# q's sums of squares taken by ones-column products on TensorE in place of transposes, in a gated delta rule layer

## What is computed

```python
qkv = jax.nn.silu(causal_depthwise_conv(qkv, w_conv_qkv[i]))      # 4 taps
q, k, v = jnp.split(qkv, 3, axis=-1)
q, k, v = l2norm(heads(q)), l2norm(heads(k)), heads(v)
o_a = gated_delta_chunked(q, k, v, g_log, beta)

def l2norm(x):
    return x * lax.rsqrt(jnp.sum(x * x, axis=-1, keepdims=True) + EPS)
```

## Time and profile before

| | |
|---|---|
| median of 3 runs | 2480.13 us (2479.77 to 2482.06) |
| the profiled execution | 2482.13 us, its span 2480.6 us |
| busy in the span: PE, PEld | 2424.2 us (98%), 1992.7 us (80%) |
| DVE, ACT, POOL | 1605.1 us (65%), 1152.9 us (46%), 142.3 us (6%) |
| instructions | 34230 |
| phase QKVZ | from about 481 to 984 us of the span |

### The profile page before, as it was taken

One profiled execution on the slowest core, in us unless ns is written; L12 is line 12 of the kernel. 1 busy time (PEld: TensorE's weight loads), 2 busy tenths in 40 slices (PEclk: granted clock), 3 DMA queues, 4 the chain that ended last, 5 costly groups with the idle time before them and its releaser, 6 DMA issues.

```text
span 2480.6 us, 34230 instructions
## 1 busy us (share of the span) xinstructions
PE 2424.2 (98%) x13427; PEld 1992.7 (80%) x13427; DVE 1605.1 (65%) x2181; ACT 1152.9 (46%) x1497; POOL 142.3 (6%) x259
## 2 busy tenths in 40 slices
PE   7999999999999999999999999999999999999998
PEld 6878878787778777778888788888888888888886
DVE  5799999777676766655656655655555544555554
ACT  5444444474353535343455564545444444443443
POOL 3000000011010102010000000000000000000000
PEclk9999999999999999999999999999999999999999
DMA  7566666556343435557655565656565656685563
GB/s 238 182 215 199 203 198 217 165 192 196 120 162 120 161 120 179 196 192 279 209 185 200 165 201 177 204 171 211 170 212 170 228 187 197 195 283 189 187 221 118
DMA packets 227756, 472.22 MB, mean 190 GB/s; under 512 B 12537, under 2 KB 13410, under 8 KB 226466
## 3 DMA queue, kind: packets, MB, share of 16 engines
q1 hardware_dynamic: 214082, 418.57, 51.6%
q0 software_dynamic: 13536, 51.70, 6.0%
HBM read 447.15 MB, written 23.09 MB: 190 GB/s over the span
## 4 chain that ended last, share of the span: by engine, by line
PE 56%; DVE 2%; DMA 1%; ACT 1%; POOL 0%; issue 0%; DVEq 0%; ACTq 0%; POOLq 0%
PE acc L2345 51%; PE aux L2392 1%; DVE w_lo L1477 1%; PE acc L2365 1%; PE aux L2521 1%; PE aux L2810 0%; DMA delta_branch_spill<-ol 0%; ACT w_hi L833 0%; DMA r1l<-delta_branch_spill 0%; DMA r1l<-conv_branch_spill 0%; DVE thm L2312 0%; PE aux L2815 0%; PE aux L2378 0%; PE aux L2821 0%; DVE us L1837 0%
## 5 line engine op out<-in xcount | busy, mean ns | idle before, releaser
L1477 DVE TENSOR_TENSOR w_lo<-raw,w_hi 128x1024 fp32r<-128x1024 f32 x790 | 965.7, 1225 | 801.3 <-ACT w_hi L833 790.3
L833 ACT CAST w_hi<-raw 128x1024 fp32r<-128x1024 f32 x790 | 826.7, 1049 | 1169.2 <-PE acc L2345 1160.9
L2345 PE MATMUL acc<-w_hi,r1h 128*128 128x512 f32 x1904 | 755.2, 397 | 10.9 <-DVE r1l L1562 4.1
L2345 PE MATMUL acc<-w_lo,r1h 128*128 128x512 f32 x1904 | 740.1, 389 | 0.0
L2345 PE MATMUL acc<-w_hi,r1l 128*128 128x512 f32 x1904 | 740.1, 389 | 0.0
L2345 PE MATMUL acc<-w_hi,r2h 128*128 128x512 f32 x1208 | 473.7, 392 | 0.0
L2345 PE MATMUL acc<-w_hi,r2l 128*128 128x512 f32 x1208 | 470.4, 389 | 0.0
L2345 PE MATMUL acc<-w_lo,r2h 128*128 128x512 f32 x1208 | 470.2, 389 | 0.0
L2345 PEld LDWEIGHTS acc<-w_hi,r1h 128*128 128x128 f32 x1904 | 358.5, 188 | 92.8 <-DVE r1l L1562 5.1
L2345 PEld LDWEIGHTS acc<-w_hi,r1l 128*128 128x128 f32 x1904 | 358.3, 188 | 75.3
L2345 PEld LDWEIGHTS acc<-w_lo,r1h 128*128 128x128 f32 x1904 | 358.9, 188 | 68.6
(11 more groups left out here) (473 smaller groups left out, 1466.3 us busy)
## 6 DMA issues: line engine op xcount, KB each, us to landing
raw<-in_w_in SPq DMA_DIRECT2D x264, 1024.0 KB, 5.0
raw<-in_w_out SPq DMA_DIRECT2D x32, 1024.0 KB, 5.0
raw<-in_w_br_b SPq DMA_DIRECT2D x16, 1024.0 KB, 5.1
raw<-in_w_br_a SPq DMA_DIRECT2D x16, 1024.0 KB, 6.8
raw<-in_w_ple_gate SPq DMA_DIRECT2D x16, 1024.0 KB, 5.1
raw<-in_w_o_mla SPq DMA_DIRECT2D x16, 1024.0 KB, 5.1
raw<-in_w_o_conv SPq DMA_DIRECT2D x16, 1024.0 KB, 5.0
raw<-in_w_q_b SPq DMA_DIRECT2D x8, 1024.0 KB, 5.1
```

The costliest lines, as they stand in the source:

```text
L833: nc.scalar.copy(w_hi[:, h % HL, 0:n], raw[:, k % RAW, x * HALF:x * HALF + n]).then_inc(hi_ready, 1)
L1477: V.tensor_tensor(w_lo[:, h % HL, 0:n], raw[:, k % RAW, x * HALF:x * HALF + n], w_hi[:, h % HL, 0:n].bitcast(F32), ALU.subtract).then_inc( ...
L2345: ins = T.matmul(acc[:, s, x, 0:n], a[:, kt0 + k, xs_], w[:, h % HL, at], start=start and k == 0 and m == 0, stop=stop and k == kts - 1 an ...
```

## The change

For q alone, the way from `qT` to the 8 sums per token is another one. ScalarE squares `qT` (channels on the partitions) into `cy` in one instruction, in the step ahead of "back". TensorE multiplies at "back": each of the 8 blocks of 128 channels x 128 tokens of squares is the stationary operand, and one column of `ones_mean` (the constant 1/D, D = 2048) is streamed. That puts the sum over the channels, divided by D, for 128 tokens into one column of bank 2. VectorE copies the 128x8 result into `dcol` a step later, and GpSimd's factor for q becomes 0.25 D. The wait of TensorE ahead of k's transposes to channels, which write the same bank, is now on `qk_square` (VectorE's copy) and no longer on ScalarE's squares. k keeps its transposes, squares and sum.

```diff
@@ GpSimd, inverse_norm
-                c.link(g.tensor_scalar(dcol[:, src], dcol[:, src], 0.25, EPS, ALU.mult, ALU.add))
+                c.link(g.tensor_scalar(dcol[:, src], dcol[:, src], 0.25 if n else 0.25 * D, EPS, ALU.mult, ALU.add))
@@ ScalarE, own
-                    if hl == back + 1 and n < 2:
-                        act.wait_ge(sem("tok_tr"), i * 2 + (n + 1))
+                    if hl == back + 1 and n == 1:
+                        act.wait_ge(sem("tok_tr"), i + 1)
...
+                    if hl == back - 1 and n == 0:
+                        act.wait_ge(sem("s_ready"), i * 2 + 1)
+                        sig(A(cy[:].rearrange("p h n -> p (h n)"), qT[:].rearrange("p h n -> p (h n)"), ACT.Square), "q_squares", i + 1)
@@ VectorE, own
-                    if hl == back + 2 and n < 2:
-                        dve.wait_ge(sem("tok_ready"), i * 2 + (n + 1))
+                    if hl == back + 1 and n == 0:
+                        dve.wait_ge(sem("q_sums"), i + 1)
+                        sig(V.tensor_copy(col(8), X[:, 2, 0:TC2]), "qk_square", i * 2 + 1)
+                    if hl == back + 2 and n == 1:
+                        dve.wait_ge(sem("tok_ready"), i + 1)
@@ TensorE, own
                         if n == 1:
-                            pe.wait_ge(sem("tok_ready"), i * 2 + 1)
+                            pe.wait_ge(sem("qk_square"), i * 2 + 1)
                         channels_first(cols(praw), OWN_BANKS[n]).then_inc(sem("ch_tr"), 1)
-                    if hl == back and n < 2:
+                    if hl == back and n == 0:
+                        pe.wait_ge(sem("q_squares"), i + 1)
+                        for m, (x, h) in enumerate(PAIRS):
+                            ins = T.matmul(X[:, 2, m:m + 1], cy[:, h, x * P:(x + 1) * P], ones_mean[:, 0:1], start=True, stop=True)
+                        ins.then_inc(sem("q_sums"), 1)
+                    if hl == back and n == 1:
                         pe.wait_ge(sem("s_ready"), i * 2 + (n + 1))
                         for x in range(TT):
                             for h in range(GH):
-                                ins = T.transpose(X[:, 2 + x, h * DK:(h + 1) * DK], (qT, kT)[n][:, h, x * P:(x + 1) * P], ident[:])
+                                ins = T.transpose(X[:, 2 + x, h * DK:(h + 1) * DK], kT[:, h, x * P:(x + 1) * P], ident[:])
                         ins.then_inc(sem("tok_tr"), 1)
```

More of the change, by code:

```diff
@@ L1008, in own @@
                 for n, (evac, _, pad, (_, conv_end), silu, back) in enumerate(OWN_FIRST if first else OWN):
-                    if hl == back + 1 and n < 2:
-                        act.wait_ge(sem("tok_tr"), i * 2 + (n + 1))
[L1011 to L1015, removed]
+                    if hl == back + 1 and n == 1:
+                        act.wait_ge(sem("tok_tr"), i + 1)
+                        if not first:
+                            act.wait_ge(sem("k_scaled"), i)
+                        for x in range(TT):
+                            c.inc(nc.scalar.copy(ktok[:, x].rearrange("p h d -> p (h d)"), X[:, 2 + x]))
                         squares = cy[:].rearrange("p h n -> p (h n)")
@@ L1020, in own @@
                                 c.inc(ins)
-                        sig(ins, "tok_ready", i * 2 + (n + 1))
+                        sig(ins, "tok_ready", i + 1)
                         c.wait()
@@ L2499, in _ @@
             ph = PH["QKVZ"]
+            PAIRS = [(x, h) for x in range(TT) for h in range(GH)]
             def own(ph, hl, i):
@@ L2511, in own @@
                             for h in range(GH):
-                                ins = T.transpose(X[:, 2 + x, h * DK:(h + 1) * DK], (qT, kT)[n][:, h, x * P:(x + 1) * P], ident[:])
+                                ins = T.transpose(X[:, 2 + x, h * DK:(h + 1) * DK], kT[:, h, x * P:(x + 1) * P], ident[:])
                         ins.then_inc(sem("tok_tr"), 1)
-            PAIRS = [(x, h) for x in range(TT) for h in range(GH)]
             def per_chunk(bank, lhsT, rhs):
@@ L2532, in delta @@
                 if hl == 0:
-                    pe.wait_ge(sem("tok_ready"), dv(2, 2))
+                    pe.wait_ge(sem("tok_ready"), dv(1, 1))
                     per_chunk(2, columns_of(kT), columns_of(kT)).then_inc(sem("B_done"), 1)
```

## The result

The changed kernel takes 2486.66 us (median of 14 runs, 2484.23 to 2488.77) beside 2480.61 us before (14 runs): ratio 1.0022, 95% interval 1.0013 to 1.003; the medians lie 6.05 us apart. Forecast were 2481.2 us and no change. Run again in another session it took 2484.97 us beside 2481.36 (ratio 1.0017, interval 1.0008 to 1.0026). So the change is slower in both sessions, by 3.6 and 6.05 us between medians, and the two intervals together allow 2 to 7.4 us. The profiled execution took 2488.36 us, 6.23 more than that of before.

What follows compares the result with a forecast made beforehand. TensorE, busy 98% of the span, was taken to bound the kernel. Passes 1 to 3 +2.64, pass 0 nothing and the clock -1.59 gave +1.05 us, 2481.2 us against the median 2480.13, range 2479.0 to 2484.6.

Steps and rivals of the forecast that it cites:

- TensorE in passes 1 to 3: At q's step, 16 records for 8 sums cost 1.76 us against 0.87 for transposes; +2.64 us over three passes.
- ScalarE's square and VectorE in passes 1 to 3: Square makes `w_hi` 1.0 us late with 1.6 us to spare at `us`; no one waits long on VectorE; priced nothing.
- Pass 0, the wait for the square: At q's step PE starts at 544.46, 1.55 us later, its wait growing from 1.35 to 2.90 us.
- The clock: In pass 0 the fall behind `kT` goes, saving 1.59 us, and the 2.90 us wait at q's step brings none.
- The price of the other branch: Clock falls at q's step, costing 1.59 us; PE reaches `kT` 0.75 us late; +1.8 us, 2481.9; forecast with clock variants 0.85.
- If `kT` does not move: In pass 0 `kT` stays ready at 570.78, so PE's 3.27 us wait shrinks to 0.84; pass 0 nets nothing.
- Sum: Whole kernel: passes 1 to 3 +2.64, pass 0 nothing, clock -1.59, giving +1.05 us, 2481.2 us against the median.

Runs made afterwards that it cites:

- a kernel of its own: The new way in passes 1 to 3 alone, pass 0 keeping q's transposes, against the changed kernel; 2484.81 us, ratio 1.0016 to the kernel before.
- one record: Sums in passes 1 to 3 as float32r products of squares rounded on writing, pass 0 keeping transposes; 2481.90 us beside 2481.48 before, ratio 1.0003.
- the doubled sums: Eight float32 sums of passes 1 to 3 made twice in a row, pass 0 keeping transposes; 2494.34 us beside 2481.36 before, ratio 1.0048.

## Why the prediction was wrong

- *TensorE in passes 1 to 3*, +2.64: right. Two records an instruction, 0.11 us each; measured 3 x 0.89 in the trace, +3.3 us as a kernel of its own, nothing left with one record.
- *ScalarE's square and VectorE in passes 1 to 3*, nothing: right, no new wait.
- *Pass 0, the wait for the square*: the sums started where they were forecast to (544.46). The wait was 3.28 us and not 2.90, since PE had run dry 0.38 us earlier in this trace; in the second trace it was 2.83 us.
- *The clock*: this step failed. "The nearest row is the wait of 2.95 us at 986.50, after which the clock stayed at 1.00. I take that, and keep the other". It fell in all four traces with a wait of 2.8 us or more at q's step. The row chosen was one draw of a thing that goes either way: the same DMA wait comes with a fall in six traces of twelve, and it was luck that the one trace at hand had none. The other row at hand, the 3.27 us before `kT`, comes with one in each of the four traces that have it (3.1 to 3.5 us). Why q's step and `kT` went one way in every trace and the DMA wait did not is open.
- *The price of the other branch*, +1.8 us in all: too low, and this term is what put the time of the first session outside the range. I took the 1.59 us that a fall had cost behind `kT`, where large products follow the wait. Here one-column records followed. They ran at half rate themselves (3.4 us for 1.8) and did not bring the clock back, so the products behind ran slow too: 4.4 us. Three things say that these records kept the clock down: with the transposes in their place, the same wait and the fall at the same point, the low spell was 3.4 us where it was 6.8 with the sums; the three spells with sums in pass 0 are 6.8, 6.8 and 10.2 us, while of the fifteen at waits with other work behind them, from 540 to 1010 us of the twelve traces, fourteen are 3.4 us; and the doubled sums bring the clock down at full load. The one spell of 6.8 us with transposes says that the price is not a fixed one, and each kernel here has one or two traces.
- *"If `kT` does not move"*: it moved by 2.7 us, because the slow products held back ACT's `w_hi` at 553.45, and with it `luh` and all behind it, where the prediction had ACT level again before `luh`. PE was later still, so this was not what bound.
- *Sum*: forecast +1.05; the traces give +2.3 for pass 0 in place of -1.6, and +2.7 for the rest as forecast: +5.0. The medians say +3.6 and +6.05. Part of what lies between is again the clock: over the 25 runs of the two sessions, those with a mean granted clock of 0.994 or less (4) took 2488.2 us on average, those with 0.995 (10) 2486.6, those with 0.996 (11) 2485.0, and the first session has 4 of its 14 runs in the last group, the second 7 of its 11. Which spells made them, no single trace can say. Over the kernel before in its own session, +3.6 us would lie inside the range that was given (2484.6 is 4.5 above 2480.13), +6.05 does not.

## What to carry to other kernels

A matmul in plain float32 was two loads and two matmuls here where a transpose was one of each, and at the full clock each record took 0.11 us with 1, 2 or 128 columns streamed. So a sum over a column of ones does not get cheaper than transposing by streaming one column: count the loads. Round the operand on writing where its precision allows, or count the records. And where TensorE has a wait of near 3 us, look at what stands right behind it: with transposes and large products the clock was back after 3.4 us in fourteen falls of fifteen here, with sixteen one-column records behind the wait after 6.8 to 10.2 us. So put such records where the stream ahead of and behind them is dense, and not too many in a row: sixteen passed at the full clock, thirty-two did not.

## What was not expected of the hardware

Thirty-two one-column records in a row (3.6 us at full clock) brought the granted clock from 1.00 to 0.50 with PE 100% busy before, in and after them, in all three passes of the one trace that has them; sixteen (1.8 us) did not, in 17 groups of five traces. The Trainium skill, "TensorE: Matmul & The Clock Gate", section "What's actually happening", says that the clock is set by how busy the PE has been recently. The falls at waits of 2.8 us agree with that; the falls at the doubled sums do not, if busy is what the profile calls busy, since that read 100% there, and the measurement decides. Waits as short as 1.9 us (for `kT`) and 2.0 and 2.5 us (for `uinv`) were followed by a fall, while half of the 2.9 us waits for the DMA were not.
